# First attention layer: scores as two 128-row products of split operands in place of one f32 product over 64 rows

## The chip, the cores and the metric

The kernel is one program on one core of a Trainium2 chip. The metric is the time on the device of one execution, in microseconds (us); smaller is better. The engines are TensorE (PE in the profile; PEld is its weight load), VectorE (DVE), ScalarE (ACT), GpSimd (POOL) and SyncE (SP), which issues DMAs.

## What is computed

Two attention and feed-forward blocks over 1024 tokens of width 1024, then a state-space and convolution block. The part that matters here is the first layer's attention: 16 query heads of 64 columns in four groups of four, each group with one key head and one value head. Each query sees the keys at most 128 away.

```python
def windowed_gqa(h, w_in, w_out, sink):
    qkv = h @ w_in
    q = qkv[..., :dq].reshape(b, s, A_KV_HEADS, gq, HEAD_DIM)      # 4 groups of 4 heads of 64
    k = qkv[..., dq:dq + dk].reshape(b, s, A_KV_HEADS, HEAD_DIM)
    v = qkv[..., dq + dk:].reshape(b, s, A_KV_HEADS, HEAD_DIM)
    o, _ = banded_attention(q, k, v, A_HALF_WINDOW, slopes, 1, sink.reshape(A_KV_HEADS, gq))
    return o.reshape(b, s, A_OUT) @ w_out

# banded_attention, per head: s = q k^T / 8 - slope * |distance|, masked;
# m = max(s, sink); p = exp(s - m); o = p v / (sum(p) + exp(sink - m))
```

## The kernel before

**Numbers in two parts.** The large products run in fp32r, a form of float32 that TensorE multiplies with fewer bits. So that nothing is lost, each operand is kept as a high part (ScalarE copies it into an fp32r tile) and a low part (VectorE subtracts the high part from the whole), and a product is made as high x high + high x low + low x high, three fp32r products into the same place in PSUM (`project_chunk`, L1500 to L1502). Some products stay in plain f32, without parts: the scores (L1593), the transposes (L1605) and the outputs (L1621).

**Units and turns.** The first layer has four units u = 0 to 3, one for each key head with its four query heads. A unit has eight turns n = 0 to 7, one for each tile of 128 queries; t = 8u + n counts them all. A turn sees up to three tiles of keys, 384 columns, and 256 in the first and the last turn of a unit. In a turn the four heads go in two pairs. `scores(t, pair)` makes the scores of a pair of heads. Both heads of a pair lie in the same tile of queries, one in rows 0 to 63 and one in rows 64 to 127, and the keys are kept twice, once in each half of the rows; so the two products of a pair use different halves of TensorE's rows. In the trace an f32 product of scores or outputs has two records, an fp32r product and a transpose one.

VectorE adds the bias and takes the minimum of the negated scores (`biased`, L3451), ScalarE makes exponentials (`exponentials`, L2549), VectorE divides (`normalised`, L3473), TensorE transposes (`turn`, L1605), ScalarE copies the turned tiles (`turned_copy`, L2562), TensorE multiplies with the values (`outputs`, L1621), and VectorE copies the result out (L3490).

**The next unit's projection** is woven between: `project(u + 1, ...)` puts six of 48 chunks into each turn, three products of 512 columns per chunk. Its results go to two PSUM banks by turns, columns 0 to 511 and 512 to 1023, in this order: keys and values (kv) of the first half of the tokens, kv of the second, q0 (queries of pair 0) first and second half, q1 (pair 1) first and second half. q11 stands for the second half of q1, q00 for the first half of q0. `proj_ready[half]` says that a bank is full, `proj_free[half]` that it has been read. VectorE reads the kv banks (`keys_values`, L3418 and L3420: keys twice, values once), ScalarE the query banks (`queries`, L2538, one activation of 128x512 with the scale 1/8). The values are turned by TensorE (L1571) and copied by VectorE (`values`, L3429) in turn 5. For unit 0 the projection runs alone ahead of the turns, into places of its own (`first_place`).

Scores have two PSUM banks in units 0 to 2, one for each head of a pair, so pair 1 of a turn waits until `biased` has read pair 0, and pair 0 of the next turn until it has read pair 1 (`scores_read`). In unit 3, where nothing is projected, pair 1 has the projection's banks, and both pairs go out in one group.

**Each engine has its own order**, written out by hand. VectorE in turn t: `values` of the next unit (n = 5), `biased(t, 0)`, `normalised(t - 1)`, `biased(t, 1)`, `outputs(t - 2)`, `keys_values` of the next unit (n = 1 and 3), the low part of a weight tile (L3592; n = 1, 4, 7), and a piece of the modulation (L2892: two dot products of 1024 columns; every turn but n = 1, up to t = 22). In unit 3 `normalised(t - 1)` stands behind `biased(t, 1)`. ScalarE in turn t: `queries` of the next unit (n = 4: q00, n = 6: q01, n = 7: q10; and n = 0: q11 of this unit), the high part of a weight tile, `exponentials(t)`, `turned_copy(t - 1)`. GpSimd loads the tile of each modulation piece (L1162) into one buffer as soon as the piece before has been read, and makes the bias tables of the next unit but one (L1148) in between, behind the last `biased` of a unit.

## Time and profile before

| | |
|---|---|
| runs | 2567.57, 2567.78, 2569.58 us; median 2567.78 us |
| profiled execution, its own time | 2567.95 us |
| its span | 2565.9 us |
| TensorE busy | 2529.6 us (99%) |
| VectorE busy | 1970.2 us (77%) |
| ScalarE busy | 1035.0 us (40%) |
| GpSimd busy | 321.0 us (13%) |
| TensorE's granted clock | 1.00 in every stretch from 68 to 450 us |
| first keys read out of PSUM | 54.3 us |
| scores of the first layer | 68.0 to 305.4 us |
| output projection alone on TensorE | from 321.0 us |

The span lies between the first and the last instruction; the time of an execution is some 2 us more. A row of the timeline merges neighbours of one kind ("x4" are four records) and gives the start, then the length up to the last end; records of TensorE overlap, since each includes the way through the array, so the cost of one is read from start to start. In square brackets stands how long the engine had been idle before, and what ended that. The first layer's attention is a tenth of the span.

### The profile page before, as it was taken

What the parts mean: (1) busy time and instruction counts of PE and PEld (TensorE: products, weight loads), DVE (VectorE), ACT (ScalarE), POOL (GpSimd) and SP (SyncE); (2) the same over time, 40 slices, a digit from 0 to 9 for tenths busy, and PEclk for the clock granted to TensorE, in tenths of its full rate; (3) what the DMA queues carried; (4) which work ended last, traced back from release to release, by engine and by line L of the source; (5) the groups of instructions that cost most, each with busy time, mean ns of one, the idle gap of its engine ahead of it and who ended that gap; (6) DMA issues with size and microseconds to landing.
All of it is one profiled execution on the core that took longest, in us unless ns stands there. A gap on an engine that the chain in (4) does not pass through costs nothing.

```text
span 2565.9 us, 37223 instructions
## 1 busy us (share of the span) xinstructions
PE 2529.6 (99%) x12662; PEld 2018.7 (79%) x12662; DVE 1970.2 (77%) x3476; ACT 1035.0 (40%) x1946; POOL 321.0 (13%) x454
## 2 busy tenths in 40 slices
PE   8999999999999999999999999999999999999998
PEld 6666688888888888777776888888888888878987
DVE  7888757889999889845555888998999987433566
ACT  6445725343333333454446453333333343111233
POOL 2011101000000000301111200000000017971000
PEclk9999999999999999999999999999999999999999
DMA  6333231211111111222322112121111132113122
GB/s 239 116 139 124 99 107 54 62 54 61 49 53 53 57 57 45 90 84 94 99 99 108 40 43 62 50 61 57 49 57 55 59 83 74 50 42 60 34 99 82
DMA packets 182017, 192.61 MB, mean 75 GB/s; under 512 B 18353, under 2 KB 146577, under 8 KB 181490
## 3 DMA queue, kind: packets, MB, share of 16 engines
q1 hardware_dynamic: 169954, 147.48, 18.0%
q0 software_dynamic: 11952, 43.65, 5.4%
q8 instruction: 69, 1.13, 0.2%
q14 instruction: 42, 0.34, 0.0%
HBM read 177.34 MB, written 12.58 MB: 74 GB/s over the span
## 4 chain that ended last, share of the span: by engine, by line
PE 93%; DVE 4%; ACT 2%; issue 1%; DMA 1%; POOL 0%; SPq 0%; DVEq 0%
PE psum L1423 21%; PE psum L1730 10%; PE psum L1731 10%; PE psum L1732 10%; PE psum L1500 5%; PE psum L1783 4%; PE psum L1782 4%; PE psum L1786 4%; PE psum L1502 4%; PE psum L1501 4%; PE psum L1771 3%; PE psum L1593 3%; PE psum L1621 3%; PE psum L1605 3%; DVE arena L2892 1%
## 5 line engine op out<-in xcount | busy, mean ns | idle before, releaser
L3181 DVE SCALAR_TENSOR_TENSOR xT<-psum,mod,xT 128x512 f32<-128x512 f32 x504 | 356.4, 745 | 61.6 <-PE psum L1786 61.3
L2346 ACT ACTIVATE w_high<-wpair 128x512 fp32r<-128x512 f32 x240 | 146.5, 626 | 315.8 <-DVE wpair L3113 244.9
L1423 PE MATMUL psum<-hT_high,w_low 128*128 128x512 f32 x928 | 261.0, 392 | 0.2 <-DVE arena L2888 0.2
L2549 ACT ACTIVATE arena<-arena 128x256 f32<-128x256 f32 (+3 forms) x296 | 146.6, 497 | 157.3 <-DVE arena L3451 157.1
L1500 PE MATMUL psum<-hT_high,w_low 128*128 128x512 f32 x480 | 203.0, 423 | 3.4 <-DVE h_low_mix L3630 3.2
L1423 PEld LDWEIGHTS psum<-hT_high,w_low 128*128 128x128 f32 x928 | 172.9, 188 | 38.3 <-issue 2.5
L1502 PE MATMUL psum<-hT_high,w_low 128*128 128x512 f32 x480 | 189.3, 394 | 0.0
L1501 PE MATMUL psum<-h_low_mix,w_low 128*128 128x512 f32 x480 | 188.5, 393 | 0.0
L1732 PE MATMUL psum<-hT_high,w_low 128*128 128x512 f32 x480 | 186.7, 389 | 0.0
L1730 PE MATMUL psum<-hT_high,w_high 128*128 128x512 f32 x472 | 183.6, 389 | 0.0
L1731 PE MATMUL psum<-h_low,w_high 128*128 128x512 f32 x472 | 183.6, 389 | 0.0
L3099 DVE TENSOR_TENSOR w_low<-wpair,w_high 128x512 fp32r<-128x512 f32 x240 | 161.8, 682 | 2.1 <-ACT w_high L2346 1.7
L1223 POOL TENSOR_TENSOR w_high<-arena,w_high 128x512 fp32r<-128x512 f32 x2 | 2.6, 1292 | 1233.9 <-ACT w_high L2333 1233.9
L3592 DVE TENSOR_TENSOR w_low<-wpair,w_low 128x1024 fp32r<-128x1024 f32 x70 | 88.6, 1267 | 85.5 <-ACT w_low L2531 85.4
L1782 PE MATMUL psum<-hT_high,w_low 128*128 128x512 f32 x360 | 140.1, 389 | 0.0
L1423 PE MATMUL psum<-h_low_mix,w_low 128*128 128x512 f32 x448 | 135.3, 390 | 0.2 <-ACT arena L2273 0.2
L1500 PEld LDWEIGHTS psum<-hT_high,w_low 128*128 128x128 f32 x480 | 90.4, 188 | 57.1 <-issue 36.3
L2531 ACT ACTIVATE w_low<-wpair 128x1024 fp32r<-128x1024 f32 x76 | 80.0, 1054 | 130.6 <-DMA wpair<-in_w_in_dram 94.1
L2562 ACT ACTIVATE arena<-psum 128x1024 f32<-128x1024 f32 (+2 forms) x80 | 85.2, 1066 | 87.8 <-PE psum L1605 87.7
L3451 DVE CUSTOM_DVE_ANT_0 arena<-psum,arena 128x192 f32<-128x192 f32 (+2 forms) x180 | 53.8, 353 | 86.0 <-PE psum L1593 86.0
L2392 ACT ACTIVATE arena<-psum 128x512 f32<-128x512 f32 x80 | 47.9, 599 | 170.3 <-PE psum L1732 114.6
L3113 DVE TENSOR_TENSOR wpair<-wpair 128x512 f32<-128x512 f32 x160 | 109.9, 687 | 6.6
(450 smaller groups left out, 6257.5 us busy)
## 6 DMA issues: line engine op xcount, KB each, us to landing
wpair<-in_ffn_w_in_dram SPq DMA_DIRECT2D x176, 256.0 KB, 2.9
wpair<-in_ada_tiles_dram POOLq DMA_DIRECT2D x20, 1024.0 KB, 5.2
arena<-in_ffn_w_out_dram SPq DMA_DIRECT2D x80, 256.0 KB, 2.9
wpair<-in_ada_tiles_dram POOLq DMA_DIRECT2D x32, 512.0 KB, 3.6
wpair<-in_w_in_dram SPq DMA_DIRECT2D x24, 512.0 KB, 3.8
wpair<-in_b_tiles_dram SPq DMA_DIRECT2D x18, 512.0 KB, 3.3
arena<-in_ada_tiles_dram SPq DMA_DIRECT2D x8, 1024.0 KB, 15.6
wpair<-in_a_tiles_dram SPq DMA_DIRECT2D x12, 512.0 KB, 4.6
```

The source lines that it names most:

```text
L1423: mm = nc.tensor.matmul(dst[:, HALF * a:HALF * a + HALF], w(k), src(k)[:, HALF * t:HALF * t + HALF], start=first and n == 0 and w is high ...
L1500: nc.tensor.matmul(dst, high[:, k, :], hT_high[:, k, rows], start=k == 0, stop=False)
L1501: nc.tensor.matmul(dst, high[:, k, :], h_low_mix[:, k, rows], start=False, stop=False)
L1502: mm = nc.tensor.matmul(dst, low[:, k, :], hT_high[:, k, rows], start=False, stop=k == KC - 1)
L1730: nc.tensor.matmul(bank[dst], high[:, k, :], moving_high(k), start=start and k == 0, stop=False, skip_group_check=not start)
L1731: nc.tensor.matmul(bank[dst], high[:, k, :], moving_low(k), start=False, stop=False, skip_group_check=not start)
L1732: mm = nc.tensor.matmul(bank[dst], low[:, k, :], moving_high(k), start=False, stop=k == 3, skip_group_check=not start)
L1782: nc.tensor.matmul(dst, down_high[w][:, cols], hid_high[v], start=start, stop=False, skip_group_check=not start)
L2346: nc.scalar.activation(of_step(s, first_high, part_high)[name], part_raw[name], ACT.Copy).then_inc(part_high_ready, 1)
L2549: e = nc.scalar.activation(s, s, ACT.Exp, bias=stat_n[:, ti, h:h + 1], scale=-1.0, accum_out=stat_l[:, ti, h:h + 1])
L3099: nc.vector.tensor_tensor(part_low[name], part_raw[name], as_f32(high), ALU.subtract).then_inc(part_split, 1)
L3181: nc.vector.scalar_tensor_tensor(xT[:, m, rows], psum[:, HALF * j:HALF * j + HALF], mod[:, l, 40 + m:41 + m], xT[:, m, rows], ALU.mult, AL ...
```

## The change

In the first layer, queries are kept as their high part in one half of the rows and their low part in the other half: for an even head high in rows 0 to 63 and low in 64 to 127, for an odd head the other way round (`q_stack`, one tile per head, half and unit parity). The keys are kept as a tile of high parts and a tile of low parts, each of them in both halves of the rows (`k_high`, `k_low`). The scores of a head are then two fp32r products over all 128 rows with the same weights: queries' tile x keys' high, plus queries' tile x keys' low. ScalarE now makes the high parts (`key_highs`, `query_highs`), VectorE the low ones (in `keys_values`, and `query_lows`), and a query bank is free only when VectorE has read it. The second layer keeps its f32 scores. Places for the new tiles are those of the weights' and hidden layer's parts, which lie idle at that time.

```diff
+        w_high_all = w_high[:, :, :].rearrange("p s n -> p (s n)")
+        spare_half = [t4_parts[:, 1, 384:896], extra[:, 3072:3584]]
+        q_even = [gate_place[:, 0, :], gate_place[:, 1, :], w_high_all[:, 0:S], hid_high_part[:, 1, 1, :]]
+        q_odd = [w_high_all[:, S:2 * S], extra[:, 0:S], extra[:, S:2 * S]]
+        q_stack = [[[q[:, HALF * half:HALF * half + HALF] for half in range(2)] for q in heads] for heads in (q_even, q_odd)]
+        q_stack[1].append(spare_half)
+        k_high = [w_high_all[:, 2 * S:3 * S], w_high_all[:, 3 * S:4 * S]]
+        k_low = [hid_high_part[:, 1, 0, :], extra[:, 2 * S:3 * S]]
...
@@ scores(t, pair), TensorE
                 if n == 0:
-                    for half in range(2):
-                        pe.wait_ge(proj_free[half], bank_use(half, f"q{pair}{half}", u) + 1)
-                    pe.wait_ge(k_ready, 4 * (u + 1))
+                    pe.wait_ge(proj_free[0], bank_use(0, f"q{pair}0", u) + 1)
+                    if a.layer == 1:
+                        pe.wait_ge(k_ready, 4 * (u - 3))
+                if n == (4 if u in (1, 2) and pair == 1 else 0):
+                    pe.wait_ge(proj_free[1], bank_use(1, f"q{pair}1", u) + 1)
...
+                    if a.layer == 0:
+                        q = q_stack[u % 2][h][n // 4][:, P * (n % 4):P * (n % 4) + P]
+                        nc.tensor.matmul(score_place(t, h)[:, lo:hi], q, k_high[u % 2][:, key + lo:key + hi], start=True, stop=False)
+                        nc.tensor.matmul(score_place(t, h)[:, lo:hi], q, k_low[u % 2][:, key + lo:key + hi], start=False, stop=True).then_inc(scores_ready, 1)
+                        continue
...
@@ ScalarE
+            def key_highs(u, half):
+
+                act.wait_ge(proj_ready[half], bank_use(half, f"kv{half}", u) + 1)
+                rows = slice(HALF * half, HALF * half + HALF)
+                nc.scalar.activation(k_high[u % 2][0:DH, rows], psum[0:DH, rows], ACT.Copy)
+                nc.scalar.activation(k_high[u % 2][DH:P, rows], psum[0:DH, rows], ACT.Copy).then_inc(k_high_ready, 1)
+
+            def query_highs(u, m, half):
+
+                act.wait_ge(proj_ready[half], bank_use(half, f"q{m}{half}", u) + 1)
+                src = psum[:, HALF * half:HALF * half + HALF] if u else first_place(f"q{m}", half)
+                nc.scalar.activation(q_stack[u % 2][2 * m][half][0:DH, :], src[0:DH, :], ACT.Copy, scale=1 / 8)
+                nc.scalar.activation(q_stack[u % 2][2 * m + 1][half][DH:P, :], src[DH:P, :], ACT.Copy, scale=1 / 8).then_inc(q_high_ready, 1)
...
                 for t in range(8 * first, 8 * last + 1):
                     u, n = t // 8, t % 8
                     if u + 1 < last and n in (4, 6, 7):
-                        queries(u + 1, int(n == 7), int(n == 6))
+                        (query_highs if u + 1 < 4 else queries)(u + 1, int(n == 7), int(n == 6))
                     if first < u < last and n == 0:
-                        queries(u, 1, 1)
+                        (query_highs if u < 4 else queries)(u, 1, 1)
+                    if u + 1 < min(last, 4) and n in (1, 3):
+                        key_highs(u + 1, n // 2)
...
@@ keys_values(u, half), VectorE
+                if a.layer == 0:
+                    rows = slice(HALF * half, HALF * half + HALF)
+                    dve.wait_ge(k_high_ready, 2 * u + half + 1)
+                    for row in (0, DH):
+                        nc.vector.tensor_tensor(k_low[u % 2][row:row + DH, rows], src[0:DH, :], as_f32(k_high[u % 2][0:DH, rows]), ALU.subtract)
+                    nc.vector.tensor_copy(lay["vT"][0:DH, rows], src[DH:P, :]).then_inc(proj_free[half], 1)
+                    return
...
+            def query_lows(u, m, half):
+
+                dve.wait_ge(q_high_ready, 4 * u + 2 * m + half + 1)
+                src = psum[:, HALF * half:HALF * half + HALF] if u else first_place(f"q{m}", half)
+                first, second = q_stack[u % 2][2 * m][half], q_stack[u % 2][2 * m + 1][half]
+                nc.vector.scalar_tensor_tensor(first[DH:P, :], src[0:DH, :], 1 / 8, as_f32(first[0:DH, :]), ALU.mult, ALU.subtract)
+                nc.vector.scalar_tensor_tensor(second[0:DH, :], src[DH:P, :], 1 / 8, as_f32(second[DH:P, :]), ALU.mult, ALU.subtract).then_inc(
+                    proj_free[half], 1)
...
                     if t < 8 * last:
                         biased(t, 0)
+                    if u + 1 < min(last, 4) and n in (4, 6, 7):
+                        query_lows(u + 1, int(n == 7), int(n == 6))
+                    if t == 24:
+                        query_lows(u, 1, 1)
                     if first == 0 and 8 * first < t < 8 * last - 8:
                         normalised(t - 1)
...
+                    if t in (8, 16):
+                        query_lows(u, 1, 1)
```

For unit 0, ahead of the turns, ScalarE makes the high parts of both halves of the keys and of q0, and after the high part of a weight tile those of q1; VectorE makes the low parts in the same order, those of q1 last, behind the low part of that weight tile and ahead of the first `biased`.

## Rows read from the trace of the kernel before

**Rows 1.** The page, parts 1 and 5: busy, count; mean ns; idle, releaser.

```profile
PE 2529.6 (99%) x12662; PEld 2018.7 (79%) x12662; DVE 1970.2 (77%) x3476; ACT 1035.0 (40%) x1946; POOL 321.0 (13%) x454
...
L3181 DVE SCALAR_TENSOR_TENSOR xT<-psum,mod,xT 128x512 f32<-128x512 f32 x504 | 356.4, 745 | 61.6 <-PE psum L1786 61.3
```

**Rows 2.** Windows: us, then busy us of each engine (instructions); clock, DMA.

```profile
76.40:145.20 68.80, 68.75 (x381) 45.72 (x380) 59.44 (x166) 34.80 (x87) 10.76 (x11) 1.00 0.37 130
145.20:215.40 70.20, 70.20 (x394) 46.80 (x393) 59.88 (x169) 35.54 (x88) 10.77 (x11) 1.00 0.37 128
```

**Rows 3.** Timeline of TensorE, turn 4: start, length, engine, line, operation.

```profile
99.20 0.92 PE L1593 MATMUL psum<-arena 64*128 64x384 f32 x4
100.05 0.50 PE L1500 MATMUL psum<-hT_high,w_low 128*128 128x512 f32 x1
100.39 0.39 PE L1501 MATMUL psum<-h_low_mix,w_low 128*128 128x512 f32 x1
...
102.00 0.39 PE L1502 MATMUL psum<-hT_high,w_low 128*128 128x512 f32 x1
102.32 0.92 PE L1593 MATMUL psum<-arena 64*128 64x384 f32 x4
103.16 1.51 PE L1621 MATMUL psum<-arena 128*64 128x256 f32 x12
```

**Rows 4.** Timeline of TensorE, a turn of unit 3.

```profile
296.07 1.56 PE L1593 MATMUL psum<-arena 64*128 64x384 f32 x8
297.56 1.53 PE L1605 MATMUL psum<-ident,hT 128*128 128x128 f32 x12
```

**Rows 5.** Timeline of VectorE, turns 1 to 24; in brackets the idle time before.

```profile
73.99 1.28 DVE L2892 CUSTOM_DVE_ANT_0 wpair<-wpair,arena,vec 128x1024 f32<-128x1024 f32 x1 [1.21 <-DMA wpair<-in_ada_tiles_dram]
...
161.46 0.62 DVE L3451 CUSTOM_DVE_ANT_0 arena<-psum,arena,less_sink 128x384 f32<-128x384 f32 x1 [1.45 <-PE psum L1593]
...
178.80 0.69 DVE L3429 COPY arena<-psum 128x512 f32<-128x512 f32 x1
180.29 0.62 DVE L3451 CUSTOM_DVE_ANT_0 arena<-psum,arena,less_sink 128x384 f32<-128x384 f32 x1 [0.80 <-PE psum L1593]
...
180.83 0.61 DVE L3451 CUSTOM_DVE_ANT_0 arena<-psum,arena,less_sink 128x384 f32<-128x384 f32 x1
...
189.29 0.62 DVE L3451 CUSTOM_DVE_ANT_0 arena<-psum,arena,less_sink 128x384 f32<-128x384 f32 x1 [1.70 <-PE psum L1593]
...
198.07 0.48 DVE L3451 CUSTOM_DVE_ANT_0 arena<-psum,arena,less_sink 128x256 f32<-128x256 f32 x1 [1.48 <-PE psum L1593]
...
212.97 1.28 DVE L2892 CUSTOM_DVE_ANT_0 wpair<-wpair,arena,vec 128x1024 f32<-128x1024 f32 x1 [1.66 <-DMA wpair<-in_ada_tiles_dram]
...
276.86 0.48 DVE L3451 CUSTOM_DVE_ANT_0 hT<-psum,arena,less_sink 128x256 f32<-128x256 f32 x1 [3.92 <-PE psum L1593]
```

**Rows 6.** Timeline of ScalarE, copies of queries of units 0 and 3.

```profile
67.46 1.28 ACT L2538 ACTIVATE arena<-psum 128x512 f32<-128x512 f32 x2 [4.98 <-PE psum L1502]
...
277.44 0.59 ACT L2538 ACTIVATE arena<-psum 128x512 f32<-128x512 f32 x1
```

**Rows 7.** Timeline of TensorE, score groups of turns 1 and 24.

```profile
77.08 1.45 PE L1593 MATMUL psum<-arena 64*128 64x384 f32 x4
...
278.13 2.57 PE L1593 MATMUL psum<-arena 64*128 64x256 f32 x12 [1.44 <-issue]
```

**Rows 8.** Timeline of TensorE, the second layer's fp32r products of 256 columns.

```profile
1410.18 0.28 PE L1950 MATMUL psum<-w_high,hT_high 128*128 128x256 f32 x1
...
1411.84 0.28 PE L1950 MATMUL psum<-w_high,hT_high 128*128 128x256 f32 x1
```

**Rows 9.** One line each: duration ns min/median/max, first and last start.

```profile
L2538 ACT ACTIVATE arena<-psum x40: 579/593/600, 56.4 to 1379.2; 128x512 f32<-128x512 f32 x40
...
L3418 DVE COPY arena<-psum x40: 661/683/685, 54.3 to 1351.0; 64x512 f32<-64x512 f32 x40
```

**Rows 10.** Timeline of GpSimd, bias tables of unit 3.

```profile
201.86 5.93 POOL L1148 TENSOR_SCALAR arena<-arena 128x384 f32<-128x384 f32 x4 [4.26 <-DVE arena L3451]
```

More of the change, by code:

```diff
@@ L1565, in turn_values @@
                 pe.wait_ge(proj_free[0], bank_use(0, "v", u))
-                pe.wait_ge(proj_free[1], bank_use(1, "kv1", u) + {0: 2, 4: 3}.get(u, 1))
+                pe.wait_ge(proj_free[1], bank_use(1, "kv1", u) + (3 if u == 4 else 1))
                 if u == 4:
@@ L2565, in attention @@
                 if first == 0:
-                    tile_highs(("q1", first))
-                    queries(first, 0, 1)
-                queries(first, 0, 0)
-                tile_highs(("kv", first + 1))
-                queries(first, 1, 0)
-                if first == 0:
-                    queries(first, 1, 1)
+                    tile_highs(("q1", 0))
+                    for half in range(2):
+                        key_highs(0, half)
+                    for half in range(2):
+                        query_highs(0, 0, half)
+                    tile_highs(("kv", 1))
+                    for half in range(2):
+                        query_highs(0, 1, half)
+                else:
+                    queries(first, 0, 0)
+                    tile_highs(("kv", first + 1))
+                    queries(first, 1, 0)
                 if first == 4:
@@ L3497, in attention @@
                     keys_values(first, 1)
+                    for half in range(2):
+                        query_lows(0, 0, half)
                 values(first)
                 tile_lows(("kv", first + 1))
+                if first == 0:
+                    for half in range(2):
+                        query_lows(0, 1, half)
                 for t in range(8 * first, 8 * last + 3):
```

6 lines of the change are left out of this document (4 added, 2 removed).

## The prediction

> **What bounds the kernel now.** I read the page first: TensorE is busy for 2529.6 of 2565.9 us, VectorE for 1970.2 [rows 1]. The whole-span shares do not decide this case, because the change touches only the first attention layer, from about 54 us (first keys out of PSUM) to about 317 us (its outputs are done). So I asked for the busy time of each engine in stretches that start and end at the same point of VectorE's work in consecutive units of eight turns [rows 2]. In the one of unit 1, 70.20 us long, TensorE is busy all 70.20 us. VectorE is busy 59.88 us and idle 10.3 us, ScalarE is busy 35.54 us. The reader is to see that TensorE sets the pace of units 0 to 2, and that VectorE is only 10.3 us per unit away from setting it.
>
> Next the timeline of TensorE in one turn [rows 3]: a score pair behind the transposes, nine projection products, the other score pair, the output products. A score group of 384 columns holds TensorE for 0.85 us (99.20 to 100.05), and the first projection product behind it takes 0.34 us to the next start where the others take 0.23, so 0.11 more. The second pair has 0.09 us of gap ahead (102.00 plus 0.23 is 102.23, the pair starts at 102.32) and 0.84 us of its own. In unit 3, where both pairs go out in one group, eight records take 1.49 us (296.07 to 297.56) [rows 4]. So four more records cost 0.64 us, and each group has 0.21 us on top, whatever its length: the drain of row halves.
>
> Then the timeline of VectorE through unit 1 [rows 5]: it stands idle for the scores at 180.29, 189.29 and 198.07 us (0.80, 1.70, 1.48 us) and for a DMA at 212.97 (1.66 us). These waits are where added VectorE work could hide. Last, the hand-over to unit 3: ScalarE, right behind a turned copy, starts the copy of q11 (queries of pair 1, second half) at 277.44 and takes 0.59 us [rows 6], and only then, at 278.13, TensorE goes on with scores, after standing 1.44 us [rows 7].
>
> **The change on TensorE.** Removed: per head one f32 product over 64 rows (two records). Added: per head two fp32r products over 128 rows with 384 (or 256) columns. The layer has no such product of 384 columns now. Its neighbours are the projection at 512 columns, one per 0.23 us (seven steps from 100.39 to 102.00) [rows 3], and an fp32r product of 256 columns with two summands per place, one per 0.119 us (14 steps in 1.66 us) [rows 8]. A line through both gives 0.1745 us at 384; the bounds are 0.119 and 0.23. Pair 0 now: 0.85 + 0.11 = 0.96 us; then: 0.11 (first after f32 work) + 4 x 0.1745 = 0.81; saved 0.15. Pair 1 now: 0.09 + 0.84 = 0.93; then: 0.70 + 0.09 ahead of the outputs = 0.79; saved 0.14. The two turns of a unit with 256 columns save as much, since two thirds of 0.64, 0.43 us of streaming, become 4 x 0.119 = 0.48 and the drain goes likewise. So 0.29 us per turn, 2.3 per unit, 7.0 over the 24 turns. In unit 3 the eight products take 8 x 0.1745 + 0.11 = 1.51 against 1.49: nothing.
>
> A rule speaks against the change. The Trainium skill, page "TensorEngine Tiling (Array Packing)", section "Theoretical Speedup", gives up to 2x for contractions of 64 rows in two tiles, which the new form gives up. The Trainium skill's page "FP8 and Floating Point Precision", section "TensorE Precision Notes", counts four passes for true fp32. By both, a pair of heads streams four passes now (two heads side by side) and four then, so streaming saves nothing; an estimate from these pages is zero but for the drain. The rows agree: 0.64 against 0.70 us, and what is saved is the fixed 0.21 us.
>
> **The change on ScalarE.** Per unit the high parts of the keys are four activations of 64x512, and queries take eight in place of four. The nearest row is 0.59 us for 128x512 [rows 9]; since length sets it I take the same. That is 8 more, 4.7 us per unit, on an engine with 34 us idle per unit in units 0 to 2 [rows 2]: free, except where someone waits for it.
>
> **The change on VectorE.** Keys: two copies become two subtractions with the same count; a copy of 64x512 from PSUM takes 0.68 us [rows 9], the nearest two-source operation from PSUM 0.707 us (356.4 us over 504, 128x512) [rows 1], so 0.1 us more per unit. Query low parts: eight new operations of 64x512 per unit, 8 x 0.707 = 5.7 us. Lower bound 0.54 us (the cadence of the biased minimum over 384 columns [rows 5]); the upper bound is 1.0 us, well into the 1.28 that a two-source operation takes for twice the columns [rows 5]. I take 0.707, a row of the same length and kind. Together 5.8 us per unit against 10.3 us idle. TensorE wants a unit of 70.2 - 2.3 = 67.9 us, VectorE then works 59.9 + 5.8 = 65.7 us: 2.2 us of air, and it doesn't lie where it is wanted.
>
> **Where the saving goes.** In turns n = 4, 6 and 7 a low part stands (1.4 us each, 4.2 together) between the two halves of the biased minimum, ahead of the normalising. The waits at n = 5, 6 and 7, behind them, are 0.80 + 1.70 + 1.48 = 4.0 us [rows 5]. So from n = 4 on VectorE has no idle time left, it is the pace, and TensorE can't run ahead of it by more than two score banks. Before n = 4 one wait of 1.45 us can be taken back (161.46), limited by what TensorE has saved by then, 3 turns x 0.29 and the 0.35 us, half a group, by which the first head's scores are there earlier (two products instead of four interleaved records): 1.2, less 0.1 for the keys, 1.1 us gained per unit. The fourth low part (q11, at n = 0) lies in the 1.66 us for the DMA and is free. That DMA does not move by itself: GpSimd makes the bias tables for 5.93 us behind the last biased minimum of the unit [rows 10], and its queue issues the DMA only after them. Unit 0 gives less, 0.6 us: at its start the q1 queries are ready at 67.46 us [rows 6], and take 2 x 1.15 us of high parts and 2 x 1.4 us of low parts where two copies took 1.28. The projection behind them starts 1.4 us late. But piece 0 of the modulation waits for its DMA until 73.99 us [rows 5], and TensorE then stalls on VectorE at 77.08 in any case (four records over 1.45 us) [rows 7]; the delay ends there. Sum at the end of unit 2: 0.6 + 1.1 + 1.1 = 2.8 us, and TensorE a further 0.6 ahead, since VectorE is idle 3.92 us there [rows 5].
>
> At turn 24 part of it goes back. Scores of pair 1 need all of q11. Now: turned copy, one activation of 0.59. Then: two high parts (1.15) and two low parts (1.4), 1.95 us more, with nothing beside it on TensorE. What is late next is the whole of unit 3. Left: 3.4 - 1.95 = 1.5 us.
>
> No other stage changes: layer 1 keeps its products and waits (its key counter only starts at zero), and no DMA is added or moved in the queues of SP or GpSimd.
>
> The profiled execution took 2567.95 us, beside the median of 2567.78; the sum is 2567.9 - 1.5 = 2566.4 us.
>
> **The rivals.**
> *TensorE's saving comes through.* If the low parts are cheaper (near 0.54 us, 1.3 us less per unit) or the waits line up better, VectorE keeps up: 7.0 - 1.95 = 5.05 us, 2562.8; with the earlier first head at unit 3's start, up to 0.7 more. For it: 2.2 us of air per unit. Against it: the bunching in n = 4, 6, 7. Chance 0.20.
> *Hand-overs cost.* Each query half now passes ScalarE, then VectorE, before its bank is free; if the start's 1.4 us are not swallowed and n = 5 stalls the projection (values wait behind the low parts), the gain of 2.8 becomes nothing while the 1.95 stay: 2569.9. For it: the values copy at 178.80 ends 0.8 us ahead of the need [rows 5]. Chance 0.14.
> *Slower: VectorE becomes the bound.* At 1.0 us each the low parts take 2.3 us more per unit; from 0.85 us on (1.1 / 8 above 0.707) no unit gains. Three units: +7, minus 1.5, 2573.3. For it: writes of one row half from the other are in no row. Against it: the copies of keys into rows 64 to 127 take what the others do (661 to 685 ns over both) [rows 9]. Chance 0.08.
> *The product does not get cheaper.* At the bound of 0.23 a pair costs 0.07 us more: +3.6 us over 24 turns, +1.8 in four of unit 3's turns (8 x 0.23 + 0.11 against 1.49), +1.95 at turn 24, 2575.3. Against it: the 256-column row at 0.119 [rows 8]. Chance 0.06.
> My own case has 0.52, and by itself a range of 2564.5 to 2568.
>
> **How the numbers follow.** 0.2% of 2567.8 is 5.1 us, about what a measurement of this kernel can tell from no change. Faster than 2562.6 is a little over half of the first rival: 0.12. Slower than 2572.9 is a little over half of the last two: 0.08. The rest, 0.80, is within. The range takes in the first rival's point and the second: 2562 to 2571.
>
> **What the new profile would show.** Score groups of 0.70 us (four records, one per 0.17); VectorE's idle time in a unit down from 10.3 to about 3 us, with its waits at n = 5 and 6 gone; two-source operations of 64x512 near 0.7 us, 32 of them for queries and 16 for keys; the step from the last turned copy of unit 2 to the scores of pair 1 up from 0.7 to 2.6 us. The stretch 76.4 to 278 us should shrink by some 1 to 2 us only. It would be wrong if VectorE still shows its waits, or if TensorE shows new ones in units 0 to 2.

## The result and the profile after

The changed kernel takes 2576.78 us (median of 9 runs, 2573.42 to 2578.93) beside 2569.81 for the kernel before (9 runs, 2567.57 to 2572.09): a ratio of 1.0026, 95% interval 1.0018 to 1.0035, so it is slower, by 6.7 us. A second series gave 1.0024 (1.0015 to 1.0033). Forecast was 2566.4, with 2562 to 2571 as the range. Ratios below are each to the kernel before in runs on the same chip.

The page of the changed kernel, its parts 1 and 5, beside [rows 1]:

```profile
PE 2526.2 (98%) x12662; PEld 2044.0 (79%) x12662; DVE 1991.4 (77%) x3508; ACT 1054.6 (41%) x1978; POOL 319.3 (12%) x454
...
L1511 PE MATMUL psum<-hT_high,w_low 128*128 128x512 f32 x480 | 201.3, 419 | 6.7 <-DVE h_low_mix L3696 2.5
```

TensorE is busy less than before and the kernel is longer: its idle time in the span goes from 36.3 to 51.0 us. Those are new waits of TensorE. The projection's first line shows 6.7 us of idle time ahead of it; the same line of the kernel before (L1500) had 3.4.

The unit of eight turns from the first transposes of turn 8 to those of turn 16, in the changed kernel (the kernel before took 70.19 us from the same point to the same point, with VectorE busy 59.87 and ScalarE 35.54, as in the second of [rows 2]); columns as there:

```profile
152.81:224.09 71.28, 68.05 (x393) 52.14 (x392) 64.92 (x175) 40.37 (x97) 10.35 (x11) 1.00 0.35 124
```

TensorE is now idle 3.2 us per unit. Before, it was never idle here. The waits of TensorE from 80 to 284 us, in the changed kernel (engine, line, who ended the wait; us in total, times, longest):

```profile
PE psum L1607 <- DVE extra L3474: 5.2, 1, 5.2
PE psum L1607 <- DVE arena L3506: 3.5, 4, 1.0
PE psum L1623 <- DVE arena L3528: 1.5, 3, 0.5
PE psum L1511 <- DVE w_low L3658: 1.4, 2, 0.7
PE psum L1511 <- DVE arena L3484: 0.9, 3, 0.3
```

and the same view of the kernel before:

```profile
PE psum L1593 <- issue: 1.4, 1, 1.4
PE psum L1605 <- DVE arena L3473: 0.6, 1, 0.6
```

The last four lines of the first list, 7.3 us, lie in units 0 to 2: scores wait for the place that the biased minimum frees (L3506), transposes for normalised rows (L3528), and the projection for a weight tile's low part (L3658) and for VectorE's copies of values (L3484). The first line is the hand-over to unit 3. Both kinds have to be explained.

Where the time arises, read from the start of the same instructions in both traces (after minus before): +0.1 us at turn 2 (97.80 and 97.90), -0.7 at turn 6, +1.1 at turn 7, +1.95 at turn 8, +0.5 at turn 14, +3.0 at turn 16, +1.7 at turn 22, +5.8 at turn 23, +6.6 at turn 31. So the change gains inside a unit, gives back more at its end, and loses 4 to 5 us more at turns 23 and 24. After the layer only small steps follow, and one of 3.2 us late in the program, which is treated under the clock below.

### The profile page after: what moved, and what is told of

It reads as the page before. It is cut to its first block, busy times and chain, and to the rows that moved or that the text cites. A ratio compares the mean times of both kernels' runs of the same rounds, so it can differ in the third digit from the quotient of the medians.

```text
span 2577.2 us, 37283 instructions
## 1 busy us (share of the span) xinstructions
PE 2526.2 (98%) x12662; PEld 2044.0 (79%) x12662; DVE 1991.4 (77%) x3508; ACT 1054.6 (41%) x1978; POOL 319.3 (12%) x454
## 4 chain that ended last, share of the span: by engine, by line
PE 86%; DVE 8%; ACT 3%; DMA 2%; issue 1%; POOL 0%; SPq 0%; DVEq 0%
PE psum L1434 20%; PE psum L1748 10%; PE psum L1749 10%; PE psum L1750 10%; PE psum L1801 4%; PE psum L1804 4%; PE psum L1800 4%; PE psum L1511 4%; PE psum L1513 3%; PE psum L1512 3%; PE psum L1789 3%; PE psum L1639 2%; PE psum L1623 2%; PE psum L1611 1%; DMA wpair<-in_ada_tiles_dram 1%
## 5 line engine op out<-in xcount | busy, mean ns | idle before, releaser
L3658 DVE TENSOR_TENSOR w_low<-wpair,w_low 128x1024 fp32r<-128x1024 f32 x70 | 89.5, 1280 | 85.3 <-ACT w_low L2549 85.0
L3506 DVE CUSTOM_DVE_ANT_0 arena<-psum,arena 128x192 f32<-128x192 f32 (+2 forms) x180 | 53.8, 353 | 88.2 <-PE psum L1611 88.2
```

## The experiments

**Two products, no split.** First half of the change alone. The kernel before, with the two fp32r products over 128 rows; queries are copied once and keys twice, as before. It leaves out the low parts, and the heads of a pair are not kept apart. The edit, shortened (as are all the edits below):

```
-  nc.tensor.matmul(score, q[64 rows], k[64 rows], start=True, stop=True)
+  nc.tensor.matmul(score, q_stack[128 rows], k_high[128 rows], start=True, stop=False)
+  nc.tensor.matmul(score, q_stack[128 rows], k_high[128 rows], start=False, stop=True)
```

> The kernel before, with the scores of the first layer as two fp32r products over 128 rows, and nothing split: ScalarE copies a query bank once (128x512) into an fp32r tile that both heads of a pair read, VectorE copies the keys twice into an fp32r tile that both products read, so TensorE streams exactly what the changed kernel streams. Left out: the low parts, and the separation of the two heads. Theory (the product itself is cheaper, 0.29 us a turn): about 7 us less than before, ratio 0.9970 to 0.9980, TensorE's transposes of turn 22 start 6 to 7 us earlier. Rival (the wider product costs TensorE as much as the pair of half-row products): ratio 1.000, the transposes of turn 22 within 1 us of before.

Measured: 2558.75 us, ratio 0.9957 (0.9943 to 0.9970), so 11 us faster. The unit has 66.56 us in place of 70.19 with TensorE busy all of it:

```profile
147.41:213.97 66.56, 66.56 (x393) 52.35 (x392) 59.25 (x167) 35.42 (x89) 10.87 (x11) 1.00 0.37 132
```

The form of the product is worth more than I had worked out: 3.63 us per unit, 0.45 us per turn on average and not 0.29. The split must cost 17 to 18 us to turn 11 gained into 6.7 lost.

**The split, no two products.** Second half alone. The changed kernel with all its high and low parts, but the score is one 64-row f32 product of the high parts; the low parts are left out of the scores.

```
-  nc.tensor.matmul(score, q, k_high, start=True, stop=False)
-  nc.tensor.matmul(score, q, k_low, start=False, stop=True)
+  nc.tensor.matmul(score, as_f32(q)[64 rows], as_f32(k_high)[64 rows], start=True, stop=True)
```

> The changed kernel, with its high and low parts made where it makes them, but each score product again one f32 product over 64 rows, of the high parts. Left out: the low parts from the products. Theory (the loss is the way of the queries through ScalarE and then VectorE): it keeps all of the loss and has none of TensorE's saving, 11 to 14 us over before, ratio 1.0043 to 1.0055. Rival (the loss comes from the wide products, by the clock or by their drain): within 2 us of before.

Measured: 2581.89 us, ratio 1.0046 (1.0032 to 1.0060), period of the unit 72.48 us. The split alone costs 12 us. The two halves alone give +12 and -11, and together +6.7, not +1: with the split in place only 5 us of the products' 11 arrive. In the unit TensorE is busy 71.2 of 72.5 us here and 68.05 of 71.28 in the changed kernel: its idle time rises from 1.3 to 3.2 us, so part of what the products save turns into waits for VectorE.

**ScalarE's last query half ahead of the turned copy.** One step of the hand-over. In the changed kernel, ScalarE makes the high parts of unit 3's q11 in turn 23, ahead of turned copy 22.

> The changed kernel, with ScalarE's high parts of the last query half (q11 of unit 3) ahead of the turned copy of turn 22 instead of behind it. Theory (the 5.2 us that TensorE stands in turn 24 are the chain exponentials, turned copy, high parts, low parts): the stand shrinks by the turned copy, 1.3 to 1.5 us, to about 3.8 us, and the time by as much (ratio to before about 1.0020). Rival (turned copy is only moved behind, and the transposed tile is late next): nothing gained.

Measured: 2574.16 us, ratio 1.0018 (1.0009 to 1.0027). TensorE's stand before the scores of pair 1 fell from 5.20 to 3.87 us, by 1.33, which is the step of the turned copy and not more. It is a third of what the stand had grown (from 1.44 us). The interval of the ratio overlaps that of the changed kernel (1.0018 to 1.0035), so here the stand is the evidence, and not the time.

**All steps in another order.** The same work as the changed kernel. ScalarE makes the query highs in turns 3, 5, 6 and 7 between exponentials and turned copy; VectorE makes the lows at the end of the same turns, behind the modulation piece, no longer between the two biased pairs.

```
-  if u + 1 < last and n in (4, 6, 7): query_highs(...)     # ScalarE, start of the turn
+  if u + 1 < min(last, 4) and n in (3, 5, 6, 7): query_highs(...)     # behind exponentials(t)
-  if u + 1 < min(last, 4) and n in (4, 6, 7): query_lows(...)     # VectorE, behind biased(t, 0)
+  if u + 1 < min(last, 4) and n in (3, 5, 6, 7): query_lows(...)     # end of the turn
```

> The changed kernel with the same work in another order. ScalarE makes the high parts of a query half between the exponentials and the turned copy of turns 3, 5, 6 and 7, as soon as its bank is full; VectorE makes the low parts at the end of the same turns, behind the modulation piece, and no longer between the halves of the biased minimum. Theory A (the order: VectorE waited for ScalarE's late high parts and pushed the normalising and the next weight tile behind them): TensorE's stalls at the turn of units and the stand at turn 24 go, the products' saving stays, 3 to 6 us less than before, ratio 0.9977 to 0.9990. Theory B (the amount: 5.8 us more on VectorE per unit): it stays at or above before, ratio 1.000 or more.

Measured: 2568.03 us, ratio 0.9990 (0.9981 to 0.9999). Nine of the 17 to 18 us that the split costs come back, with no instruction fewer. Its unit:

```profile
150.88:220.24 69.36, 67.41 (x394) 52.36 (x393) 64.65 (x175) 40.49 (x96) 10.33 (x11) 1.00 0.38 129
```

VectorE is busy for 64.65 us, as much as in the changed kernel, and the period is still 2.8 us above that of the kernel without the split (69.36 less 66.56). Whether that rest is VectorE's amount or again an order is what the next four runs ask.

**VectorE's low parts alone moved.** ScalarE keeps the order of the changed kernel.

```
-  query_lows(...)     # n in (4, 6, 7), behind biased(t, 0), ahead of normalised(t - 1) and biased(t, 1)
+  query_lows(...)     # n in (4, 6, 7), behind biased(t, 1)
```

> The changed kernel with one thing moved: in the last turns of a unit (n = 4, 6, 7) VectorE makes the low parts of the next unit's queries behind the second biased pair of the turn, no longer between the two pairs. ScalarE's order is that of the changed kernel. Theory 1 (order at the unit's end: in turns 7 and 15 VectorE stands 1.48 us in the middle of the turn for a high part that ScalarE makes only behind its exponentials, and with that the second biased pair, the normalised rows and the weight tile come late): the second pair no longer waits, so the turn of n = 7 loses about 1 to 1.5 us per unit, 3 to 4 us in all: 2572 to 2574, ratio to the kernel before 1.001 to 1.0015. Theory 2 (the loss lies in the amount of VectorE's work alone, and where its stands lie does not matter): as the changed kernel, 2576 to 2577, ratio 1.0026. Theory 3 (the low parts come too late for the scores of the next unit when they stand behind the pair): slower than the changed kernel, above 2578.

Measured: 2568.75 us, ratio 1.0002 (0.9993 to 1.0011). One call moved behind two others takes back 6 us, more than the 3 to 4 expected; the period falls from 71.28 to 68.85 us, 7 us over three units if all were alike. VectorE is busy 64.98 us in the unit, as in the changed kernel (64.92); its idle time falls from 6.36 to 3.87 us. The second theory (only the amount counts) is out. The hand-over stays bad: a stand of 3.67 us. The unit is even 0.5 us shorter than that of the reordered kernel, so what the other order has over this one (ratios 0.9990 and 1.0002, whose intervals overlap) isn't inside the unit.

**Less work on VectorE.** The reordered kernel, with the values' copies (vT and v) of units 1 to 3 on ScalarE. One of the two:

```
-  nc.vector.tensor_copy(lay["vT"][0:DH, rows], src[DH:P, :])
+  nc.scalar.activation(LAY[0]["vT"][0:DH, rows], psum[DH:P, rows], ACT.Copy)
```

> The reordered kernel (e4) with two kinds of copies of units 1 to 3 taken from VectorE to ScalarE: the copies of the values' half out of the projection and the copy of the turned values, about 2.1 us of VectorE per unit by the 0.5 to 0.6 us that such a copy takes. Theory 1 (behind the right order VectorE's amount is the pace: it is busy 64.65 of the unit's 69.36 us, where the kernel with two products and no split has a period of 66.56): about 2 us per unit come back, 6 us in all less a part at the hand-over: 2562 to 2564, ratio 0.997 to 0.9975. Theory 2 (what is left against the kernel without the split is waits for the order, the amount costs nothing): as e4, 2568, ratio 0.999. Theory 3 (ScalarE's queue becomes late, since the copies stand ahead of its exponentials): slower than e4, 2570 or more.

Measured: 2563.03 us, ratio 0.9977 (0.9968 to 0.9987): 3 to 4 us faster than the reordered kernel, by intervals that just overlap, with a unit that is 0.80 us shorter:

```profile
150.01:218.57 68.56, 67.34 (x393) 52.23 (x392) 63.19 (x172) 42.22 (x99) 10.33 (x11) 1.00 0.38 131
```

**More work on VectorE.** The reordered kernel, with the first low-part subtraction of each query half of units 1 to 3 done twice.

```
+  if u:
+      after(nc.vector.scalar_tensor_tensor(first[DH:P, :], src[0:DH, :], 1 / 8, as_f32(first[0:DH, :]), ALU.mult, ALU.subtract))
```

> The dose the other way: e4 with the first of the two low-part subtractions of each query half of units 1 to 3 done twice, 4 more VectorE operations of 0.69 us per unit, each with a wait of VectorE for its own one. Same result. Theory 1 (VectorE's amount is the pace): 2.8 us per unit and some 0.1 us for each own wait, 6 to 9 us in all: 2574 to 2577, ratio 1.0015 to 1.0025. Theory 2 (amount costs nothing as long as the order is right: 4.7 us of a unit VectorE is idle): 2568 to 2570, ratio 0.999 to 1.000.

Measured: 2575.07 us, ratio 1.0025 (1.0015 to 1.0035). Its unit:

```profile
152.75:224.92 72.17, 67.84 (x394) 52.20 (x392) 67.50 (x179) 40.31 (x96) 10.33 (x11) 1.00 0.36 125
```

VectorE is busy 2.85 us more (67.50 less 64.65) and the period is 2.81 us longer: one for one. Downwards the copies' 1.46 us gave 0.80, about half. From the reordered kernel upwards VectorE is the pace of this unit. Not all of the 9 us between the two ratios is this: at the hand-over TensorE stood 2.05 us in place of 1.35, and its clock went down behind it (see below).

**Still less work on VectorE.** The kernel of "less work" with the copies of the attention outputs of turns 0 to 21 on ScalarE too.

> e6 with one more kind of copy on ScalarE: the attention outputs of turns 0 to 21 out of TensorE's memory, one of about 0.42 us in each turn, 3.4 us of VectorE per unit, on top of the 2.1 us of e6. Theory 1 (VectorE's amount is the pace until TensorE's own work is, 66.6 us per unit in the kernel without the split): the unit's period falls from e4's 69.36 to between 66.6 and 67.5 us, 5 to 8 us in all: 2559 to 2563, ratio 0.9960 to 0.9975, TensorE the bound again. Theory 2 (the amount costs nothing): as e4, 2568. Theory 3 (ScalarE becomes late: its copy of the outputs stands behind the turned copy and TensorE waits for the place): at or above e4.

Measured: 2561.35 us, ratio 0.9972 (0.9961 to 0.9983). The period is 68.07 us, above the 66.6 to 67.5 expected:

```profile
148.46:216.53 68.07, 66.98 (x393) 52.39 (x392) 60.44 (x164) 44.27 (x107) 10.33 (x11) 1.00 0.37 131
```

A further 2.75 us off VectorE give 0.49. The amount has stopped being the limit. What stays is one wait of TensorE, 1.09 us ahead of the scores of pair 1 of turn 16, for the biased minimum L3528 of pair 0.

**One low part into the wait for a transfer.**

```
-  if u + 1 < min(last, 4) and n in (3, 5, 6, 7): query_lows(u + 1, int(n > 5), int(n in (5, 7)))     # end of the turn
+  if u + 1 < min(last, 4) and n in (3, 5, 7): query_lows(u + 1, int(n > 5), int(n in (5, 7)))
+  if u + 1 < min(last, 4) and n == 7: query_lows(u + 1, 1, 0)     # behind biased(t, 1)
```

> e8 with one step moved: the low parts of the third query half of the next unit are no longer made by VectorE at the end of turn n = 6, where they stand ahead of the first biased pair of n = 7 and TensorE waits 1.09 us for that pair, but in n = 7 behind its second biased pair, where e8's VectorE stands 1.44 us for a transfer of the modulation's. Theory 1 (where in the turn VectorE's added work lies decides, a stand of TensorE for a biased pair comes back in full): 0.7 to 1.1 us per unit, 2 to 3 us in all: 2558 to 2560, ratio 0.9960 to 0.9965, near the kernel with the two products and no split (0.9957). Theory 2 (the rest against that kernel is VectorE's amount, 1.2 us more per unit): as e8, ratio 0.9972.

Measured: 2562.55 us, ratio 0.9965 (0.9952 to 0.9979), which can't be told from the run above (0.9972). The period is 67.87 us and the wait that should have gone is still there, in the timeline of TensorE (pair 0 and pair 1 of turn 16):

```profile
201.06 0.36 PE L1607 MATMUL psum<-w_high,gate_place 128*128 128x256 f32 x1
...
204.96 0.35 PE L1607 MATMUL psum<-w_high 128*128 128x256 f32 x1 [1.13 <-DVE arena L3528]
```

The expectation had the wrong low part. VectorE's timeline of this run shows who stands ahead of that minimum:

```profile
197.33 0.68 DVE L3495 SCALAR_TENSOR_TENSOR w_high<-psum,w_high 64x512 fp32r<-64x512 f32 x1
...
202.90 0.68 DVE L3495 SCALAR_TENSOR_TENSOR w_high<-psum,w_high 64x512 fp32r<-64x512 f32 x1
203.60 0.69 DVE L3496 SCALAR_TENSOR_TENSOR hid_high<-psum,hid_high 64x512 fp32r<-64x512 f32 x1
204.32 0.48 DVE L3528 CUSTOM_DVE_ANT_0 arena<-psum,arena,less_sink 128x256 f32<-128x256 f32 x1
```

The moved pair is the one at 197.33 (q10), behind the second biased pair of turn 15. The pair at 202.90 is q11 at the end of turn 15 (n = 7), and that stayed; the minimum behind it at 204.32 is the first of turn 16. TensorE had made the scores of turn 16, pair 0, at 201.06. VectorE runs behind TensorE here, so an instruction's turn on VectorE isn't the turn that TensorE is in at that time; I had taken the low parts ahead of that minimum for those of n = 6. Moving the q11 pair wasn't tried.

**The hand-over alone.** The changed kernel; for unit 3 alone q11's high parts come in turn 23 ahead of the turned copy and its low parts at the end of turn 23.

> The changed kernel with the hand-over to unit 3 alone mended: the last query half of unit 3 gets its high parts from ScalarE in turn 23 behind the exponentials (ahead of the turned copy) and its low parts from VectorE at the end of turn 23, as in e4; units 1 and 2 are as in the changed kernel. Theory 1 (the hand-over cost 5.2 us of a stand where 1.4 stood before, and TensorE then works 3.6 us at the 1.2 GHz level): the stand falls to that of e4's, under 1 us, the granted clock stays at 1.00 behind it, turn 24 starts 4 to 5.5 us earlier against turn 22; 2571 to 2573, ratio 1.0005 to 1.0015, and what is left against e4 is the boundaries of units 1 and 2. Theory 2 (a late start of unit 3 is made good behind it, since its turns wait for other things too): 2575 to 2577.

Measured: 2575.52 us, ratio 1.0016 (1.0007 to 1.0025), just above the expected 1.0005 to 1.0015, and the stand, expected under 1 us (the reordered kernel, to which the expectation points, has 1.35), is 3.86:

```profile
281.75 0.51 PE L1607 MATMUL psum<-w_high,extra 128*128 128x256 f32 x1 [3.86 <-DVE extra L3476]
```

So the place of q11 explains 1.34 of 5.20 us, as in the third run, and the rest comes from earlier. That rest is worked out below.

**Both kernels again, for a second profile.**

> The changed kernel once more, on the chip of the last two, with a second profile. All theories: 2576 to 2577, ratio 1.0026. Open is whether the stretch of 6.5 us at the 1.2 GHz level at 2159 us, in which TensorE was busy throughout and which the kernel before did not show, comes again at the same place: if it belongs to the change, yes, at the same length; if it is the chip's own, at another length or not at all.

> The kernel before once more, for a second profile of it: 2568 to 2571. If the late stretch at the 1.2 GHz level is the chip's own, it can show here too; if it belongs to the change, it is absent again.

Measured: the changed kernel 2577.37 us, ratio 1.0024 (1.0015 to 1.0033), the kernel before 2570.06 us in one run. The late stretch came again in the changed kernel at the same place and length, and the kernel before now showed one of half that length: so it isn't the change's alone. The last section has the rows.

## Why the prediction was wrong

The step that failed is the one called "Where the saving goes". It charged a low part with 1.4 us, let VectorE's idle time of 4.0 us take most of that up, and came to 1.1 us gained in unit 1; that VectorE would have to wait for the high part itself, with work for TensorE queued behind, was put at nothing. The unit took 71.28 us in place of 70.19, 1.1 us lost. The other term that was too small is the hand-over to unit 3, 1.95 us forecast and 5.0 measured.

**The product's time was right, its saving was not.** Forecast: one 384-column fp32r product per 0.1745 us. The changed kernel's TensorE, same turn as [rows 3]:

```profile
97.90 1.47 PE L1623 MATMUL psum<-ident,arena 128*128 128x128 f32 x12
99.13 0.42 PE L1607 MATMUL psum<-w_high,gate_place 128*128 128x384 f32 x1
99.38 0.34 PE L1608 MATMUL psum<-hid_high,gate_place 128*128 128x384 f32 x1
99.56 0.34 PE L1607 MATMUL psum<-w_high,gate_place 128*128 128x384 f32 x1
99.74 0.33 PE L1608 MATMUL psum<-hid_high,gate_place 128*128 128x384 f32 x1
99.91 0.39 PE L1511 MATMUL psum<-hT_high,w_low 128*128 128x512 f32 x1
...
102.00 0.33 PE L1607 MATMUL psum<-w_high 128*128 128x384 f32 x1
...
102.78 1.52 PE L1639 MATMUL psum<-arena 128*64 128x256 f32 x12
```

Starts are 0.17 to 0.18 us apart, and 0.25 behind the first. Pair 1 holds TensorE for 0.78 us (102.00 to 102.78) against 0.93: 0.15 saved where 0.14 was forecast. Pair 0 holds it for 0.78 (99.13 to 99.91) against 0.96, 0.18 saved where 0.15 was forecast. The term left out stands ahead of it: in the kernel before, the twelve transposes begin at 97.80 and the first score at 99.20, 1.40 us; now it is 1.23 (97.90 to 99.13). So 0.17 us were lost on this side of the row halves too, and I had counted a gap ahead of them only for pair 1. In sum 0.17 + 0.18 + 0.15 = 0.50 us in this turn, against 0.29; the kernel with the products alone bears it out with 11 us against the forecast 7.0. The Trainium skill's page "TensorEngine Tiling (Array Packing)", section "Theoretical Speedup", gives the gain of two 64-row tiles over the whole array and puts no number on the switch between them. The trace differs from it: here giving up the two tiles gained 0.50 us in a turn.

**The low parts' own time was right.** Forecast 0.707 us; they take 0.68 and 0.69, 32 of them. ScalarE's high parts take 0.59 as assumed. The rival in which they take 1.0 us named the right side (slower, 2573.3 us) and the wrong cause.

**The start was right.** TensorE waited 1.6 us for the low parts of q1 and turn 2 began 0.1 us later than before; the delay was swallowed.

**"From n = 4 on VectorE has no idle time left, it is the pace": the right observation, with the wrong sum.** The forecast gave each low part its 1.4 us of VectorE and stopped. It left out what the low part itself waits for. ScalarE makes the high part of n = 7 where the query copy stood, behind exponentials and a turned copy; VectorE never waited for that copy, but its low part waits for the high part. VectorE of the changed kernel at n = 7 of unit 1:

```profile
201.56 0.68 DVE L3473 SCALAR_TENSOR_TENSOR w_high<-psum,w_high 64x512 fp32r<-64x512 f32 x1 [1.48 <-ACT hid_high L2563]
202.26 0.69 DVE L3474 SCALAR_TENSOR_TENSOR hid_high<-psum,hid_high 64x512 fp32r<-64x512 f32 x1
...
203.39 1.41 DVE L3528 TENSOR_SCALAR arena<-arena 128x384 f32<-128x384 f32 x4
204.83 0.49 DVE L3506 CUSTOM_DVE_ANT_0 arena<-psum,arena,less_sink 128x256 f32<-128x256 f32 x1
...
206.18 1.23 DVE L3658 TENSOR_TENSOR w_low<-wpair,w_low 128x1024 fp32r<-128x1024 f32 x1
...
210.23 0.47 DVE L3506 CUSTOM_DVE_ANT_0 arena<-psum,arena,less_sink 128x256 f32<-128x256 f32 x1
```

and TensorE in the same stretch:

```profile
204.86 1.53 PE L1623 MATMUL psum<-ident,arena 128*128 128x128 f32 x12 [0.51 <-DVE arena L3528]
...
207.56 0.47 PE L1511 MATMUL psum<-hT_high,w_low 128*128 128x512 f32 x1 [0.70 <-DVE w_low L3658]
...
210.86 0.36 PE L1607 MATMUL psum<-w_high 128*128 128x256 f32 x1 [0.98 <-DVE arena L3506]
```

The reader sees VectorE idle for 1.48 us with the normalising (203.39), the second biased minimum, a weight tile's low part (206.18) and the first minimum of turn 16 (210.23) in its queue behind. TensorE waits for three of them in turn: its transposes 0.51 us for the normalised rows, the projection 0.70 for the weight tile, the scores of turn 16, pair 1, 0.98 for that minimum. So an engine that was said to have no idle time stands idle on its critical stretch, and what is queued behind is late by the wait and the 1.4 us of the low part. On the chip: low parts behind the second minimum, ratio 1.0002, instead of between the two, 1.0026. In that run VectorE waits nowhere in the unit for a high part. It takes the wait and the 1.4 us away from there together, so what each of them costs alone is not shown. The prediction asked where a low part's duration goes and not what is queued behind its wait.

**A late minimum also makes a transfer late.** The prediction said of the DMA at n = 0 that it does not move by itself, and laid the fourth low part in that wait. But GpSimd starts the bias tables behind the last biased minimum of a unit and issues that transfer behind them. The issue came 3.4 us behind the start of turn 14's transposes in the kernel before (207.74 and 204.39), 6.4 us behind it in the changed one (211.28 and 204.86), and 3.8 with the low parts behind the second minimum (205.70 and 201.92). VectorE's waits for these transfers from 80 to 278 us are 3.3 us before, 7.3 changed, and 2.5 in the kernel with the low parts moved (there from 78 to 276 us). Part of what that move gave can come this way; no run takes it apart.

**The amount cost more than "2.2 us of air" said.** TensorE wanted 66.56 us per unit and not 67.9, and VectorE was busy 64.9. There were 1.6 us of air, where VectorE's waits for a DMA alone were 2.9 us in the changed kernel's unit, of the 6.4 it was idle (forecast: about 3). The runs with one kind of copy less and with one subtraction more give 0.8 us per unit for 1.46 and 2.81 for 2.85: above the reordered kernel's 64.65 us of VectorE each microsecond comes in full, below them about half of one.

**The hand-over: forecast +1.95 us, measured +5.0.** From the start of turn 22's transposes to that of turn 24's the kernel before needs 10.63 us (274.58 to 285.21) and the changed one 15.62 (276.27 to 291.89). VectorE of the changed kernel:

```profile
272.98 0.68 DVE L3473 SCALAR_TENSOR_TENSOR extra<-psum,extra 64x512 fp32r<-64x512 f32 x1 [1.48 <-ACT t_parts L2563]
...
276.66 0.48 DVE L3506 CUSTOM_DVE_ANT_0 arena<-psum,arena,less_sink 128x256 f32<-128x256 f32 x1
...
281.94 0.68 DVE L3473 SCALAR_TENSOR_TENSOR extra<-psum,extra 64x512 fp32r<-64x512 f32 x1 [2.82 <-ACT extra L2563]
```

ScalarE:

```profile
277.18 0.51 ACT L2581 ACTIVATE arena<-arena 128x256 f32<-128x256 f32 x1 [4.24 <-DVE arena L3506]
...
279.38 1.45 ACT L2594 ACTIVATE arena<-psum 128x1536 f32<-128x1536 f32 x1
280.72 0.58 ACT L2562 ACTIVATE extra<-psum 64x512 fp32r<-64x512 f32 x1
281.31 0.59 ACT L2563 ACTIVATE extra<-psum 64x512 fp32r<-64x512 f32 x1
```

and TensorE:

```profile
283.47 0.55 PE L1607 MATMUL psum<-w_high,extra 128*128 128x256 f32 x1 [5.20 <-DVE extra L3474]
...
285.75 0.52 PE L1607 MATMUL psum<-w_high,extra 128*128 128x384 f32 x1
286.06 0.52 PE L1608 MATMUL psum<-extra 128*128 128x384 f32 x1
...
287.02 1.91 PE L1623 MATMUL psum<-ident,arena 128*128 128x128 f32 x8
```

The chain is: last biased minimum of unit 2 (ends 277.1), exponentials, turned copy, two high parts, two low parts, scores. The two parts on which I put 1.95 us are right in length. But the chain starts late: in the kernel before VectorE ended that minimum 2.6 us ahead of turn 22's transposes (271.95 and 274.58), in the changed one 0.9 us behind them (277.14 and 276.27), a shift of 3.5 us. VectorE's lateness at the end of a unit, which had no term in my sum, meets here a chain that TensorE can't cover. The three stands of 5.20, 3.87 or 3.86 (q11 ahead of the turned copy) and 1.35 us (the reordered kernel, whose minimum ends 1.6 us ahead of turn 22's transposes) split it: 1.3 for the turned copy and 2.5 for the lateness. The hand-over run and the reordered one make q11's parts at the same places and differ in the units ahead; 2.5 us is also what the minimum moved between them.

**And the clock went down behind the stand.** Windows of the changed kernel; the column ahead of the last two is the granted clock:

```profile
278.30:283.40 5.10, 0.00 (x0) 0.00 (x0) 2.19 (x6) 3.57 (x8) 0.00 (x0) 0.88 1.05 403
283.40:288.60 5.20, 5.13 (x20) 4.99 (x20) 4.25 (x17) 2.18 (x9) 0.40 (x2) 0.50 1.03 414
288.60:291.90 3.30, 3.30 (x23) 2.32 (x22) 2.64 (x11) 2.93 (x5) 0.20 (x1) 0.93 0.77 225
```

In the first TensorE has no instruction at all. In the second it is granted 0.50, the 1.2 GHz level. A product of 384 columns takes 0.31 us to the next start in place of 0.17 (285.75 to 286.06), the eight transposes 1.84 (287.02 to the next start at 288.86) where the hand-over run, its clock back by then, has 0.97 (285.24 to 286.21). 5.2 us at half speed do the work of 2.6, so some 2.6 us are lost there, by an estimate from the clock alone. The kernel before has 1.00 in the same stage:

```profile
282.00:288.00 6.00, 6.00 (x45) 3.40 (x44) 5.88 (x23) 5.62 (x13) 0.80 (x4) 1.00 1.02 415
```

The kernels with a stand of 3.86 and 3.87 us also went down (granted 0.52 from 281.7 to 284.9 us in the hand-over run), the reordered one with 1.35 did not (1.00 from 275.7 to 282.8). The kernel with one subtraction more went down behind a stand of only 2.05 us (1.00 in the stand, 0.53 from 283.3 to 285.9 us behind it). The prediction had no such term.

**The sum, put right.** By ratios, in us of 2570: products -11; the split +17.7; together +6.7. Of the split, the order takes 9 (1.0026 to 0.9990), and in that the low parts' place about 6 (to 1.0002) and ScalarE's place and the hand-over about 3. VectorE's amount takes 5 (0.9990 to 0.9972). The rest, 0.9972 to 0.9957, 4 us, was not taken apart; the waits like that before turn 16's scores are 2.2 us of it. Intervals are about 0.1% each way, 2.5 us, so these are sizes and not accounts; the traces' periods (71.28, 69.36, 68.07, 66.56) put them in the same order. The fastest kernels that compute all of the reference's function are that with the values' and outputs' copies on ScalarE, 2561.35 us, 0.28% below the kernel before, and its sister with one low part moved (0.9965), which can't be told apart.

What the prediction named as proof against itself, that TensorE shows new waits in units 0 to 2, is what the trace showed first. Of its rivals, "Hand-overs cost" named the right kind of place and a third of the price. One wait that it named is there, the projection's for VectorE's copies of values, 0.9 us in three units; the other, the start, was swallowed.

## What to carry to other kernels

An added step in a three-engine hand-over costs three things: its length, the wait for its own input where it stands, and the lateness that reaches the next barrier. Look at what is queued behind it on its engine and put it where its input is long ready, behind what the bounding engine waits for; here that was one call moved, and 6 us. When an engine has under 2 us of air in 67, count every microsecond put on it as a full one, and look for another engine's idle time, here ScalarE's. And judge an instruction that switches the tiling of the array by both sides of the switch.

## What the runs showed of the hardware

Stretches at the 1.2 GHz level also come where the profile has TensorE busy throughout, and differ between executions of one program. Late in the program, over the same products, the kernel before had none in the first profile (1.00 throughout 2145 to 2170 us) and one in the second; the changed kernel had a longer one in both. Windows of the first kernel's second profile:

```profile
2154.00:2160.00 6.00, 6.00 (x21) 4.75 (x20) 3.12 (x13) 0.21 (x1) 4.71 (x17) 0.72 0.01 3
```

and of the changed kernel's first and second:

```profile
2157.00:2168.00 11.00, 11.00 (x51) 9.46 (x51) 3.81 (x17) 0.42 (x2) 8.39 (x33) 0.69 0.17 49
```

```profile
2159.00:2167.00 8.00, 8.00 (x30) 6.76 (x30) 3.76 (x17) 0.42 (x2) 6.17 (x22) 0.57 0.17 51
```

The loss by these shares is 6 x 0.28 = 1.7 us, 11 x 0.31 = 3.4 and 8 x 0.43 = 3.4; aligned by instruction, the changed kernel falls back 3.2 us there against the kernel before in the first pair of profiles and 1.6 in the second. It does not follow the time of a kernel: the hand-over run, slower than the kernel before, has none there (1.00 from 2140 to 2170 us), and the run with one low part moved, 0.35% faster, loses as much as the changed kernel (0.62 over 9 us, 3.4 us).

What TensorE does ahead of them is the same each time: 32 products of a single column. In the changed kernel's first profile, and in that of the kernel before, which kept its clock:

```profile
2156.65 4.18 PE L2071 MATMUL psum<-ones,arena 128*128 128x1 f32 x32
```

```profile
2148.89 3.63 PE L2053 MATMUL psum<-ones,arena 128*128 128x1 f32 x32
```

Of the 14 profiles of this case 12 have the lower level there, and in each of them it starts inside this group or at most 1.3 us behind its end, and lasts 3.4 to 6.9 us. Two, the first of the kernel before and the hand-over run, have the same group and keep 1.00. Why some executions go down and others don't stays open, and no run left the group out. Whether the change makes the stretch longer, two profiles of each kernel can't tell.

These stretches go with the spread of some 4 us among a kernel's runs: in the 21 runs of the kernel before beside the first four experiments, the two with a mean granted clock of 0.996 take 2571.4 us in the mean, the six with 0.997 take 2570.3, the two with 0.999 take 2568.5. The profile from which the prediction was made had 0.999, so the spans of the first two profiles are 11.3 us apart where the medians are 7.

Writing from one row half into the other costs nothing that shows: the query lows, all across, take 0.68 and 0.69 us, and the key lows (L3458), half of them across, 0.67 to 0.69.
